# Where the gathered expert steps stand beside the dense top-16 searches

## The chip, the cores and the metric

The kernel runs as one program on 1 core of a Trainium2 chip. A core has five engines with a queue of instructions each: TensorE (PE in the profile, its weight loads PEld), VectorE (DVE), ScalarE (ACT), GpSimd (POOL) and SyncE (SP). 16 DMA engines move data beside them. An engine takes its instructions strictly in their written order and waits on semaphores, so a wait also holds back all that stands behind it. The metric is the device time of one execution in microseconds.

## The reference

One layer of a diffusion backbone runs over 128 context tokens and 512 latent tokens of width 1024, five tiles of 128 tokens. A token mixer comes first. The change lies in the second half of the layer, PEER, a retrieval over 16384 one-neuron experts:

```
q = (xb @ w_query).reshape(t, 8, 2, 128)                  # 8 heads
s = einsum('thik,hink->thin', q, sub_keys)                # 2 x 128 scores a head
v_half, i_half = top_k(s, 16)                             # top 16 of each half
cand = v_half[:, :, 0, :, None] + v_half[:, :, 1, None, :]
top_v, top_pos = top_k(cand, 16)                          # top 16 of the 256 sums
idx, g = <expert numbers>, softmax(top_v)
act = gelu(einsum('thkd,td->thk', expert_u[idx], xb))
out = einsum('thk,thkd->td', g * act, expert_v[idx])
```

So each token has 128 picks: 8 heads of 16. The result is normalised, gated and added to the token.

## The kernel before, in words

**Two ways of doing the picks.** The context tile (tile 0) and latent tiles 1 and 2 (`APART`) are *gathered*. For every pick, GpSimd issues an indirect DMA that brings one row of `expert_u` for each of the 128 tokens (128 x 4 KB, 0.524 MB), VectorE takes its dot product with the token (`u_dot`), and later the row of `expert_v` comes and VectorE adds it, weighted (`v_add`). Latent tiles 3 and 4 (`WHOLE`) are *dense*. TensorE multiplies them with all of `expert_u`, streamed by SyncE as 128 blocks of 0.524 MB (`s_block`), ScalarE applies the gelu and stores (`take_s`). The gates are then built as a matrix from one-hot rows (`build`: `equal`, `weigh_i`, `build_unit`, `gate_unit`, 64 units), and TensorE multiplies with the blocks of `expert_v`.

**Steps.** The gathered tiles 1 and 2 have 2 x 128 picks. Step j of `apart_steps` on VectorE takes the dot product of pick j and, from j = 40 (`APART_LEAD`), adds the v row of pick j - 40. At j = 40, 56, 72, ... it also runs `weights` for a head, which needs ScalarE's `gates`. ASTEPS is 296. GpSimd's `rows_of_apart` issues the gathers in the same order: u row j, then v row j - 40. A row waits for its buffer: picks 0 to 31 use eight u buffers in turn; from pick 32 there are four for u rows and four for v rows. For row 32 GpSimd also waits until the context output has been stored (`out_done`), because two of the later buffers lie where that output was.

**Searches.** `top(...)` on VectorE does two top-16 searches. For head h the pair (3 * PH + h, 4 * PH + h) are the dense tiles; `topw_done` tells that all eight are finished. For gathered tiles it takes two heads at a time and releases 32 rows to GpSimd (`topk_done`). Pairs (0, 1) and (2, 3) stand between the dense searches (`APART_TOP_BESIDE`), later ones within the steps (`APART_TOP_AT`; pair (4, 5) at step 50).

**The written order around the change.** On VectorE:

```
for h in range(PH):
    top(3 * PH + h, 4 * PH + h)
    context_steps(CTX_BESIDE[h])
    if h in APART_TOP_BESIDE: top(...)
    if h == 6: result(0, pv_c, row(3, 0), 1, 0)
    apart_steps(APART_BESIDE[h])
apart_steps(SOFTMAX_AT)                  # 8
weigh_whole()
apart_steps(APART_EARLY - SOFTMAX_AT)
dve.wait_ge(s("tw_out"), 1)
build()
```

`result` finishes the context tile (L2260 to L2262) and lets ScalarE store it. ScalarE's `store(0, 1)` stands behind the take of dense block 24. `weigh_whole` normalises the dense softmax weights. It needs the exponent that ScalarE takes of them (`ew_done`, L1601 and L1602), and TensorE needs it in turn: behind dense block 46 stands `turn_tables` (L1160), which waits on `gw_done`. Behind the take of block 48 ScalarE copies the turned tables (`tw_out`). The first `equal` of the build also needs dense block 59, the build's matmuls all 64.

TensorE alternates between two banks for the dense blocks: block n waits until ScalarE has taken block n - 2. SyncE loads into six block buffers: block n is loaded once block n - 6 has been multiplied. Context picks have the same two kinds of steps (`context_steps`); their last five stand behind head 3's search.

`START_1`, the number of steps ahead of the build, is `sum(APART_BESIDE) + APART_EARLY`. From it follow the places of the later steps, of ScalarE's gates and of the second half's multiplications.

Of the kernel before, what the change touches and what calls it, by code (L numbers as in the profile page):

```python
# [184 lines left out]
ROW_NUMBER = {row: n for n, row in enumerate(ROW_ORDER)}  # L185
ASTEPS = 2 * PICKS + APART_LEAD
CTX_BESIDE = (5, 5, 5, 5, 0, 0, 0, 0)
APART_BESIDE = (0, 0, 0, 0, 8, 8, 8, 8)
APART_TOP_BESIDE = {2: (0, 1), 6: (2, 3)}
APART_TOP_AT = {16 * n - (7 if n == 6 else 14): (n, n + 1) for n in range(4, 2 * PH, 2)}  # L190
APART_EARLY = 42
SOFTMAX_AT = 8
UNITS = 64
UNIT = 4
# [21 lines left out]

START_1 = sum(APART_BESIDE) + APART_EARLY
START_BETWEEN = START_1 + sum(APART_BUILD)
# [95 lines left out]
def layer_kernel(nc, a, outs):  # L314

    y_out, st_out = outs
    with ExitStack() as ctx:
# [131 lines left out]
        def row(kind, t):  # L449
            return rows[kind][1 if t else 0]  # L450
# [47 lines left out]
        def s(name):  # L498
            if name not in S:
                S[name] = sem(name)  # L500
            return S[name]
# [705 lines left out]
        def _(act):  # L1207
# [345 lines left out]
            def tile_norm(n, src, out):  # L1553

                ch(A(out, src, ACT.Square, accum_out=pstat[:, n, 0:1]))
                A(pstat[:, n, 1:2], pstat[:, n, 0:1], ACT.Sqrt, bias=eps[:], scale=1.0 / D).then_inc(s("pv_done"), 1)
# [3 lines left out]
            def store(t, turn):  # L1560
                act.wait_ge(s("out_ready"), turn)
                nc.scalar.dma_start(yv[:, t, :], x1(t)).then_inc(s("out_done"), 16)
# [18 lines left out]
            def take_s(n, i):  # L1581

                act.wait_ge(s("s_full"), n + 1)
                if i >= HALF:
                    act.wait_ge(s("av_done"), i - HALF + 1)
                elif i == 32:
                    act.wait_ge(s("topw_done"), 2 * PH)
                elif i == 48:
                    act.wait_ge(s("u_used"), PICKS + 30)
                A(Aw[:, i % HALF, :], bank[4 + n % 2][:, 0:2 * P], ACT.Gelu_apprx_tanh).then_inc(s("s_out"), 1)  # L1590

            for n, i in enumerate(FIRST_ORDER):
                take_s(n, i)
                if n == 8:
                    act.wait_ge(s("vc_used"), PICKS)
                    tile_norm(0, pv_c, h2c)
                if n == 24:
                    store(0, 1)
                if n == 31:
                    act.wait_ge(s("topw_done"), 2 * PH)  # L1600
                    A(iotas, iota.unsqueeze(2).broadcast_to([P, P, UNIT]), ACT.Copy)  # L1601
                    A(d_w, d_w, ACT.Exp).then_inc(s("ew_done"), 1)  # L1602
                for item in APART_GATES.get(("first", n), []):
                    gates(item)
                if n == 48:
                    act.wait_ge(s("tw_full"), 1)
                    A(turned_i, bank[6][:, 0:2 * P], ACT.Copy)
                    A(turned_w[:, 1, :], bank[6][:, 2 * P:], ACT.Copy)
                    A(turned_w[:, 2, :], bank[7][:, 0:2 * P], ACT.Copy).then_inc(s("tw_out"), 1)
# [183 lines left out]
        def _(dve):  # L1793
# [521 lines left out]
# [3 lines that stand above are left out]
                if h in APART_TOP_BESIDE:  # L2318
                    top(*(PH + n for n in APART_TOP_BESIDE[h]))
                if h == 6:  # L2320
                    result(0, pv_c, row(3, 0), 1, 0)
                apart_steps(APART_BESIDE[h])
            apart_steps(SOFTMAX_AT)
# [3 lines that stand above are left out]
# [74 lines left out]
```

## Time and profile before

| | |
|---|---|
| median of 3 runs | 2661.77 us (2661.74 to 2667.35) |
| profiled execution | 2663.96 us, its span 2662.2 us |
| mean granted TensorE clock | 0.946 of full speed |
| TensorE busy | 2308.1 us (87%) |
| VectorE busy | 1822.3 us (68%) |
| GpSimd busy | 1164.0 us (44%) |
| ScalarE busy | 616.5 us (23%) |
| DMA | 702.71 MB, mean 264 GB/s |

The span runs from the first to the last instruction of the profiled execution; the execution's own time is a little longer than that. Busy shares are averages over stages with different limits. Times in the rows below are microseconds from the span's start. In a row in order of time the first number is when the instruction started and the second how long it was busy; in brackets stand the idle time of its engine just ahead of it and what ended that idle time.

### The profile page before, as it was taken

The numbers are of one execution on the slowest core, as the hardware profiler recorded it, in microseconds if no ns is written. First come the engines' busy times: TensorE is split into PE (matmuls) and PEld (weight loads), VectorE is DVE, ScalarE is ACT, GpSimd is POOL, SyncE is SP. The second block draws the span as 40 slices with busy tenths as digits, with TensorE's granted clock in tenths as the row PEclk, the third lists the DMA queues.
The fourth block names the chain that finished last, engine by engine and source line by source line (L and its number), as shares of the span: only waits on it lengthen the run. The fifth ranks groups of instructions, "written<-read, shape, count | busy, mean of one in ns | idle before, by whom it ended". The sixth has DMA issues, their size and how long they took to land.

```text
span 2662.2 us, 26319 instructions
## 1 busy us (share of the span) xinstructions
PE 2308.1 (87%) x8735; PEld 1447.0 (54%) x8735; DVE 1822.3 (68%) x3244; ACT 616.5 (23%) x1503; POOL 1164.0 (44%) x960
## 2 busy tenths in 40 slices
PE   6998888898999997999989989646899999999920
PEld 1344455444566543477578878546566666544400
DVE  2656776743100789787778996899767576767698
ACT  2215263421211113311421112168111011100010
POOL 0011222311000347676542336553547868776675
PEclk8999999999999998999999999878999999999965
DMA  9421110115184678999764779976999999999997
GB/s 361 143 79 40 32 50 31 55 40 173 64 279 163 214 302 332 352 399 415 273 259 174 267 260 362 349 278 210 357 419 383 394 378 419 355 419 392 410 388 291
DMA packets 235150, 702.71 MB, mean 264 GB/s; under 512 B 21008, under 2 KB 45712, under 8 KB 233616
## 3 DMA queue, kind: packets, MB, share of 16 engines
q0 software_dynamic: 115200, 419.48, 41.4%
q1 hardware_dynamic: 119104, 279.06, 28.3%
q10 hardware_dynamic: 720, 2.62, 0.2%
q8 instruction: 63, 1.03, 0.1%
q14 instruction: 63, 0.52, 0.1%
HBM read 687.98 MB, written 13.11 MB: 263 GB/s over the span
## 4 chain that ended last, share of the span: by engine, by line
PE 31%; DVE 26%; POOL 14%; DMA 14%; issue 11%; ACT 3%; SPq 1%; DVEq 0%; ACTq 0%; POOLq 0%
PE bank L933 12%; DMA arena<-in_peer_v,arena 7%; POOL arena L1730 6%; POOL arena L1722 6%; PE bank L779 4%; DMA arena<-in_peer_u,arena 4%; DVE arena L2143 4%; DVE arena L2121 3%; PE bank L825 2%; DVE arena L1908 2%; PE bank L1083 2%; DVE arena L2067 2%; POOL arena L1776 2%; PE bank L734 2%; DVE arena L2064 2%
## 5 line engine op out<-in xcount | busy, mean ns | idle before, releaser
L1722 POOL DMA_INDIRECT arena<-in_peer_u,arena x384 | 500.9, 1304 | 728.0 <-DVE arena L2121 384.2
L2143 DVE SCALAR_TENSOR_TENSOR arena<-arena 128x1024 f32<-128x1024 f32 x381 | 497.5, 1306 | 137.2 <-DMA arena<-in_peer_v,arena 132.0
L2121 DVE CUSTOM_DVE_ANT_0 arena<-arena 128x1024 f32<-128x1024 f32 x384 | 474.4, 1242 | 152.1 <-DMA arena<-in_peer_u,arena 151.8
L1730 POOL DMA_INDIRECT arena<-in_peer_v,arena x384 | 451.7, 1176 | 245.2 <-DVE arena L2143 138.5
L933 PE MATMUL bank<-arena 128*128 128x512 f32 (+1 forms) x1472 | 504.6, 504 | 14.2 <-DMA arena<-in_w_in 5.1
L1153 PE MATMUL bank<-arena 128*128 128x256 f32 x2048 | 455.2, 380 | 10.8 <-ACT arena L1590 10.0
L1184 PE MATMUL bank<-arena 128*128 128x512 f32 x1024 | 453.7, 596 | 7.7 <-DMA arena<-in_peer_v 4.5
L1153 PEld LDWEIGHTS bank<-arena 128*128 128x128 f32 x2048 | 390.1, 191 | 92.2 <-issue 41.4
L933 PEld LDWEIGHTS bank<-arena 128*128 128x128 f32 x1472 | 280.6, 192 | 233.9 <-issue 199.7
L1184 PEld LDWEIGHTS bank<-arena 128*128 128x128 f32 x1024 | 195.5, 191 | 227.9 <-issue 219.3
L779 PE MATMUL bank<-arena 128*128 128x512 f32 x384 | 187.3, 636 | 5.3 <-ACT arena L1263 3.9
L1590 ACT ACTIVATE arena<-bank 128x256 f32<-128x256 f32 x128 | 48.8, 383 | 589.4 <-PE bank L1153 575.5
L1695 POOL TENSOR_TENSOR arena<-arena 128x512 f32<-128x512 f32 x40 | 43.6, 1090 | 269.1 <-ACT arena L1311 269.1
L1171 PE MATMUL bank<-arena 128*128 128x128 f32 x512 | 81.1, 316 | 79.5 <-ACT arena L1626 79.5
L779 PEld LDWEIGHTS bank<-arena 128*128 128x128 f32 x384 | 75.3, 205 | 90.5 <-issue 88.8
L1108 PE MATMUL bank<-arena 128*128 128x256 f32 x512 | 114.1, 384 | 8.2 <-ACT arena L1516 8.2
L1171 PEld LDWEIGHTS bank<-arena 128*128 128x128 f32 x512 | 72.1, 221 | 88.8 <-issue 44.5
L1908 DVE SCALAR_TENSOR_TENSOR arena<-arena,convw_sb 128x644 f32<-128x644 f32 x96 | 101.5, 1058 | 12.4 <-DVE arena L1906 2.0
L1108 PEld LDWEIGHTS bank<-arena 128*128 128x128 f32 x512 | 98.0, 193 | 21.9 <-issue 7.7
L1311 ACT ACTIVATE arena<-bank,arena 128x128 f32<-128x128 f32 x320 | 86.9, 393 | 46.7 <-PE bank L875 46.2
L1626 ACT ACTIVATE arena<-arena 128x128 f32<-128x128 bf16 x256 | 83.3, 401 | 42.3 <-DVE arena L2287 42.3
L1279 ACT ACTIVATE arena<-bank 128x512 f32<-128x512 f32 x60 | 35.2, 597 | 224.5 <-PE bank L933 218.1
(252 smaller groups left out, 2352.5 us busy)
## 6 DMA issues: line engine op xcount, KB each, us to landing
arena<-in_peer_ut SPq DMA_DIRECT2D x128, 512.0 KB, 6.5
arena<-in_peer_v SPq DMA_DIRECT2D x128, 512.0 KB, 6.5
arena<-in_w_in SPq DMA_DIRECT2D x22, 2048.0 KB, 9.1
arena<-in_w_ada SPq DMA_DIRECT2D x8, 2048.0 KB, 12.0
arena<-in_w_ssd_out SPq DMA_DIRECT2D x8, 2048.0 KB, 13.4
arena<-in_w_query SPq DMA_DIRECT2D x8, 2048.0 KB, 8.0
arena<-in_w_ada_t POOLq DMA_DIRECT2D x16, 512.0 KB, 4.5
arena<-in_w_fourier SPq DMA_DIRECT2D x4, 2048.0 KB, 7.6
```

The lines of the kernel that those rows point to most:

```text
L779: mm(bank[2][:, :], w[:, k, c0:c0 + P], hT[:, k, P:TOK], start=(k == 0), stop=(k == KT - 1), skip_group_check=True)
L933: last = mm(bank[q % 5][:, 0:cols], rows_of(k), w[:, k, :], start=(k == 0), stop=(k == k_tiles - 1))
L1108: last = mm(bank[n % 4][:, 0:2 * P], w[:, k, c0:c0 + P], h2Tp[1 - pair][:, k, :], start=(k == 0), stop=(k == KT - 1))
L1153: last = mm(bank[4 + n % 2][:, 0:2 * P], ut[:, k, :], h2Tp[1][:, k, :], start=(k == 0), stop=(k == KT - 1))
L1171: last = mm(bank[GATE_BANKS[u % 6]][:, P * t:P * t + P], hot_j[u % HOTS][:, t, :], hot_i[u % HOTS][:, t, :], start=True, stop=True)
L1184: last = mm(bank[2 * t + half][:, :], Aw[:, i % HALF, t * P:t * P + P], v[:, 512 * half:512 * half + 512], start=(i == 0), stop=(i == NKEY ...
L1311: last = A(Ee[:, e % 4, j, :], bank[d][:, j * P:(j + 1) * P], ACT.Exp, bias=ncs[:, c, ds(g * HG + 32 * d + 4 * hq + j, 1)])
L1722: nc.gpsimd.indirect_dma_start(rowbuf[slot], None, a["peer_u"], bass.IndirectOffsetOnAxis(ap=entries(IDX, k), axis=0)).then_inc(row_in[slo ...
L1730: nc.gpsimd.indirect_dma_start(rowbuf[slot], None, a["peer_v"], bass.IndirectOffsetOnAxis(ap=entries(IDX, k), axis=0)).then_inc(row_in[slo ...
L1908: last = STT(o, cin[:, i % 2, k:k + 644], w(k), o, ALU.mult, ALU.add)
L2121: V.tensor_tensor_reduce(out=rowbuf[slot], in0=rowbuf[slot], in1=h2c if item < PH else h2a[:, item // PH - 1, :], scale=1.0, scalar=0.0, o ...
L2143: STT(pv, rowbuf[slot], w, pv, ALU.mult, ALU.add).then_inc(s("vc_used"), 1)
```

## The change

Three tables of the order of work and one condition change. Four gathered steps move behind head 3's dense search and two more behind each of heads 4 to 7; 12 fewer stand behind the dense searches. The second gathered pair of heads, (2, 3), is searched at head 5 instead of head 6. ScalarE takes the dense exponent behind its take of block 39 instead of block 31. `SOFTMAX_AT` stays 8, so `weigh_whole` stands behind step 51 where it stood behind step 39. The sum `START_1` stays 74.

```diff
-APART_BESIDE = (0, 0, 0, 0, 8, 8, 8, 8)
-APART_TOP_BESIDE = {2: (0, 1), 6: (2, 3)}
+APART_BESIDE = (0, 0, 0, 4, 10, 10, 10, 10)
+APART_TOP_BESIDE = {2: (0, 1), 5: (2, 3)}
 APART_TOP_AT = {16 * n - (7 if n == 6 else 14): (n, n + 1) for n in range(4, 2 * PH, 2)}
-APART_EARLY = 42
+APART_EARLY = 30
...
-                if n == 31:
+                if n == 39:
                     act.wait_ge(s("topw_done"), 2 * PH)
                     A(iotas, iota.unsqueeze(2).broadcast_to([P, P, UNIT]), ACT.Copy)
                     A(d_w, d_w, ACT.Exp).then_inc(s("ew_done"), 1)
```

## Rows read from the trace of the kernel before

**Rows 1.** busy time by stretch (busy us and instructions of each engine, granted clock, DMA)

```profile
1558.00:1610.00 52.00, 41.97 (x186) 36.06 (x185) 49.93 (x141) 11.02 (x21) 15.85 (x11) 0.93 0.62 215
...
1752.00:1860.00 108.00, 73.70 (x468) 65.45 (x469) 107.53 (x219) 91.48 (x299) 41.13 (x32) 0.89 0.64 217
1860.00:2330.00 470.00, 459.69 (x1601) 303.04 (x1600) 327.98 (x558) 55.56 (x128) 321.80 (x255) 0.99 0.98 386
```

**Rows 2.** the same view, stretches beside and without dense block loads

```profile
1630.00:1671.00 41.00, 41.00 (x194) 36.12 (x193) 26.08 (x34) 7.63 (x18) 33.70 (x23) 1.00 1.03 418
1691.00:1713.00 22.00, 18.41 (x86) 15.86 (x84) 20.55 (x27) 2.30 (x6) 17.56 (x15) 1.00 0.90 310
1713.00:1751.00 38.00, 0.00 (x0) 0.00 (x0) 33.42 (x44) 0.00 (x0) 29.94 (x27) 0.50 0.99 365
```

**Rows 3.** order of time, ScalarE (start us, us, what, idle before and releaser)

```profile
1575.61 0.38 ACTq L1562 DMA_DIRECT2D y_out<-arena  x1
1576.05 0.66 ACT L1590 ACTIVATE arena<-bank 128x256 f32<-128x256 f32 x2 [13.85 <-DVE arena L2262]
1582.09 0.38 ACT L1590 ACTIVATE arena<-bank 128x256 f32<-128x256 f32 x1 [5.38 <-PE bank L1153]
...
1600.73 0.63 ACT L1601 ACTIVATE arena<-shape_consts 128x512 bf16<-128x512 f32 x1 [4.44 <-DVE arena L2109]
...
1709.44 0.38 ACT L1590 ACTIVATE arena<-bank 128x256 f32<-128x256 f32 x1 [3.07 <-PE bank L1153]
1752.15 4.91 ACT L1626 ACTIVATE arena<-arena 128x128 f32<-128x128 bf16 x16 [42.33 <-DVE arena L2287]
```

**Rows 4.** order of time, TensorE

```profile
1649.88 0.82 PE L1160 MATMUL bank<-shape_consts,arena 128*128 128x128 f32 x6
...
1753.56 6.67 PE L1171 MATMUL bank<-arena 128*128 128x128 f32 x40 [44.15 <-ACT arena L1626]
```

**Rows 5.** order of time, VectorE (L2121 dot product, L2143 add, L2063 search, L2287 build)

```profile
1489.30 1.28 DVE L2143 SCALAR_TENSOR_TENSOR arena<-arena 128x1024 f32<-128x1024 f32 x1 [1.74 <-DMA arena<-in_peer_v,arena]
...
1584.66 0.29 DVE L2063 MAX8 arena<-arena 128x8 f32<-128x128 f32 x1
...
1600.61 1.22 DVE L2121 CUSTOM_DVE_ANT_0 arena<-arena 128x1024 f32<-128x1024 f32 x1
...
1609.77 1.22 DVE L2121 CUSTOM_DVE_ANT_0 arena<-arena 128x1024 f32<-128x1024 f32 x1
...
1629.88 1.23 DVE L2121 CUSTOM_DVE_ANT_0 arena<-arena 128x1024 f32<-128x1024 f32 x1 [2.10 <-DMA arena<-in_peer_u,arena]
...
1668.41 1.23 DVE L2121 CUSTOM_DVE_ANT_0 arena<-arena 128x1024 f32<-128x1024 f32 x1
...
1690.85 1.22 DVE L2121 CUSTOM_DVE_ANT_0 arena<-arena 128x1024 f32<-128x1024 f32 x1
...
1751.65 0.41 DVE L2287 TENSOR_TENSOR arena<-arena 128x512 bf16<-128x512 bf16 x1
```

**Rows 6.** order of time, GpSimd (L1722 gathers of u rows, L1730 of v rows)

```profile
1483.67 1.93 POOL L1730 DMA_INDIRECT arena<-in_peer_v,arena  x1 [32.38 <-DVE arena L2143]
1485.90 1.08 POOL L1722 DMA_INDIRECT arena<-in_peer_u,arena  x1 [0.30 <-issue]
...
1537.33 1.99 POOL L1722 DMA_INDIRECT arena<-in_peer_u,arena  x1 [0.30 <-issue]
...
1543.15 0.94 POOL L1722 DMA_INDIRECT arena<-in_peer_u,arena  x1 [0.30 <-issue]
...
1604.92 1.15 POOL L1722 DMA_INDIRECT arena<-in_peer_u,arena  x1 [14.41 <-DVE arena L2121]
...
1690.01 1.74 POOL L1722 DMA_INDIRECT arena<-in_peer_u,arena  x1 [15.34 <-DVE arena L2121]
```

**Rows 7.** DMA issues, 1476 to 1500 us, then 1540 to 1610 (median us to landing)

```profile
arena<-in_peer_u,arena POOLq DMA_INDIRECT x8, 8.8
...
y_out<-arena ACTq DMA_DIRECT2D x1, 512.0 KB, 2.6
```

## The prediction

> **What bounds the kernel now.** I read the page first, then the stretches around the change, then each engine's order of time there. The page's busy shares mix stages, so the stretches say more. After 1752 us the engines build the gates (VectorE 107.5 of 108 us busy), then come 470 us at a DMA share of 0.98 [rows 1]. All work after 1752 us is in the same order with and without the change, for START_1 stays 74 (32 + 42, then 44 + 30), and every later index derives from it. So the change is worth what it moves the start of the build, and a shift there reaches the end whole.
>
> What ends last before the build? ScalarE takes the last dense block at 1709.44 and then idles 42.3 us for VectorE [rows 3]; TensorE idles 44.2 us with it [rows 4]. VectorE is the late one: its first `equal` runs at 1751.65, right after step 73 of the gathered tiles [rows 5]. Dense work has 42 us to spare, VectorE none.
>
> VectorE is late because its rows are. From 1600.61 on, nine dot products (steps 24 to 32) run without a wait, one each 1.145 us (9.16 over 8). After them each waits: step 40 starts at 1629.88 and step 50 at 1668.41 [rows 5], 3.85 us a step for 2.4 us of work. In that time the DMA moves 418 GB/s, one 0.524 MB dense block each 3.45 us plus two gathered rows a step, with VectorE busy 26 of 41 us [rows 2]. Ahead of it, from 1558 to 1610, the DMA share is only 0.62 [rows 1]. That hole is what earlier steps could fill.
>
> **The change, part by part.** Twelve steps go ahead of or between searches: four to head 3, two more each to heads 4 to 7. Eight steps then remain before `weigh_whole` as before, so it runs after step 51 instead of after step 39; the top search of step 50 (16 us) now stands ahead of it too. The GpSimd queue issues its gathers in an unchanged order. No instruction is added or removed.
>
> *Head 3, steps 0 to 3.* The last context add ends at 1490.6 [rows 5]. The first row gather is issued at 1485.90 and gathers of that stretch land 8.8 us after issue in the median [rows 7]. For the first I take 5.6 us, which is what the gather just ahead needed (issued 1483.67 [rows 6], added at 1489.30), for the next three one per 1.95 us (half the 3.85 to 3.9 us step). The fourth lands at 1497.3, so head 4's searches start near 1498.4: 7.8 us later, 4.6 of work and 3.2 of waiting. Bounds for the waiting: 0 (all landed) to 8 (8.8 us for the last, and its issue four places down).
>
> *Heads 4 and 5.* Ten steps with eight row buffers, a search of 16 us ahead of each. The ninth and tenth rows are issued while the first two are used, and must land in some 8 us; row 32 did that in under 5 us (issued 1604.92 [rows 6], used 1609.77 [rows 5]). Cost 2.3 us a head, no wait. The second gathered pair moves from head 6 to 5, but both places precede the context result, so it moves nothing else.
>
> *The context result and its store.* It had 16 steps ahead of it, now 24: 8 x 1.145 = 9.2, plus 3.2 = 12.4 us. Its store goes from 1575.61 to 1588.0. ScalarE is held there, behind dense block 24, and TensorE behind ScalarE, which idles 13.9 us now [rows 3] and 26.3 then. I cost this at nothing by itself: the 42 us of slack hide it, but it moves blocks 27 to 63 by 12.4 us.
>
> *Head 6, steps 32 and 33.* Row 32's buffer waits for the store to land, 2.6 us [rows 7]: about 1591. Issue takes up to 1.99 us beside dot products, 0.94 beside searches [rows 6]. I put the landing near 1597.5 and that of row 33 near 1599.5, so the head ends at 1600.7 against 1599.5 unhindered. Bounds 0 to 5 us.
>
> *Head 7.* A 15.95 us search (1584.66 to 1600.61 [rows 5]) ends the dense searches at 1616.6, before it was 1600.6. The exponent at block 39 runs at 1582.09 (the take of block 27 [rows 3]) + 12.4 + 12 x 3.453 = 1635.9, so it waits for nothing, where it waited 4.4 us. Steps 34 to 37 then run freely to 1621.2. Row 38 is issued at 1618.1 and lands near 1624.6, row 39 near 1626.7, row 40 near 1631. That is 1.3 us behind the present 1629.88. The steps that ran early have thus bought nothing by step 40: the hole is filled at one place and another opens under head 7's search, where only four buffers are left to prefetch into, instead of eight.
>
> *The new wait.* TensorE turns the weights after dense block 46 and needs `weigh_whole`. It passes there now at 1649.88 [rows 4]. With the change it ends block 46 at 1582.09 + 12.4 + 19 x 3.453 = 1660.1 (a take follows each 0.38 + 3.07 us). Steps 40 to 47 at 3.85 reach 1662; from there the blocks are held and steps 48 to 50 run at the 2.9 us of a time without blocks (38 us for 27 gathers is 1.41 each [rows 2]). Step 50 starts near 1667, works 2.4, searches 16.2, step 51 takes 2.4, the weights 1.2: 1689.2. TensorE stands 29 us there, with blocks 47 to 63, ScalarE's takes and every later block load queued behind it. Its slack becomes: 1689.2 + 1.2 for the turns + 17 x 3.453 = 1749.1, plus a restart. The restart is bounded by the present one, after the store: the next take waited 5.4 us where 3.07 is usual, 2.3 us more [rows 3]; if all of two blocks ran at half clock it is 7. I take 3: 1752.
>
> *Late steps.* Now VectorE needs 60.8 us from step 52 at 1690.85 to `equal` at 1751.65 [rows 5], with almost no block traffic. The first row that it needs from there is issued at 1690.01 [rows 6]. In the changed kernel it starts at 1689.2, but eleven block loads (53 to 63) fall into that stretch, over 11 x 3.453 = 38 us. A gather beside blocks takes 1.78 to 1.93 us (41 us for 23, or half a step), without them 1.47 (22 us for 15) [rows 2]. About 20 gathers x 0.4 = 7.5 us more. Below stands nothing (blocks hidden), above 11 x 1.27 = 14 us (every block's 0.524 MB at 418 GB/s added in full). I take 7.5, since the two mixed and unmixed rows are this very pair. 1689.2 + 60.8 + 7.5 = 1757.5.
>
> The Trainium skill (DMA: Bandwidth & Descriptors, Where 436 GB/s comes from) puts the HBM side of one core at about 358 GB/s. By it 38 gathers and 11 blocks (25.7 MB) would take at least 72 us here, and the build would start near 1761. The 418 GB/s over 41 us of this trace contradict it, and the row decides.
>
> **Sum.** The build starts at 1757.5, not 1751.65: +5.9 us, rounded 6. The profiled execution took 2663.96 us (span 2662.2), so 2670; that execution lies 2.2 us over the median of 2661.77, so against the median I say 2667.8 us, +0.22%.
>
> **Rivals.**
> *Issue, not traffic, sets the gathers (no change).* GpSimd is never idle for longer than its 0.30 us gap from 1690 on, and one gather takes 0.94 us beside searches and 1.99 beside dot products [rows 6]. If issue sets the rate, the late blocks are free: VectorE ends at 1750.0, TensorE at 1752, and the build starts at 1752, +0.5 us: 2662.3. Against it: beside blocks the issue itself lengthens, with VectorE less busy (26 of 41 us against 20.6 of 22). The Trainium skill (SBUF — State Buffer, SBUF: two separate sides) has VectorE lock GpSimd out of a shared port while it writes descriptors; by that rule this rival would be the likely one.
>
> *It is faster: the rows come ahead.* If steps 0 to 3, 32, 33 and 38 to 40 find rows landed, since fewer blocks have passed by then (3.6 blocks, 12.4 / 3.453, at 1.27 us are 4.6 us of traffic put off), the weights are ready near 1684. TensorE ends at 1747; if late blocks are hidden too, the build starts 5 us early: 2656.8. It decides only where the weights come before 1685, since TensorE has 63 us of work behind them whatever VectorE does.
>
> *It is much slower.* The late steps run at the mixed 3.85 us for all 22: 85 less the four buffered ones (4 x 1.45) is 79, the build starts at 1768, +16.5: 2678.
>
> *The move does nothing.* Steps before 40 are undone by waits, as above, and the new wait ends just with VectorE: within 2 us, 2662.
>
> **How the numbers follow.** Forecast 0.50, its own range +2 to +11 (2664 to 2673), of it 0.40 above 0.2%. 0.2% is 5.3 us, about what a measurement of this kernel tells from none. Issue-bound 0.20, all same. Nothing 0.05, same. Faster 0.15. Much slower 0.10, with its upper half beyond the range. Slower 0.50, same 0.35, faster 0.15. The range 2658 to 2675 leaves out about half of the faster case and most of the much slower one.
>
> **What would show it.** Right: the ScalarE store near 1588; exponent near 1636 without a wait; a TensorE gap of 25 to 32 us ahead of the turns of L1160; step 51 behind the search near 1688; last dense take near 1752, not 1709; `equal` near 1757. Wrong: a gap ahead of L1160 under 20 us (the weights come early, the faster case), late steps still at 2.8 us a piece beside block loads (issue-bound), or a difference that grows or shrinks after the build, which I hold to be none.

## The result: 0.57% slower, and the profile after

| | before | changed |
|---|---|---|
| median of 7 runs each, on one chip | 2661.77 us | 2677.43 us |
| ratio of the times, 95% interval | | 1.0057 [1.0041, 1.0073] |
| profiled execution, its span | 2663.96, 2662.2 us | 2676.04, 2674.1 us |
| `equal` of the build starts | 1751.65 us | 1767.01 us |
| last dense block taken | 1709.44 us | 1759.46 us |

The ratio is some 15 us where 6 were forecast. The direction is right, the size is not. In the trace the build starts 15.4 us later. 2.0 us of it were there before the change begins: the last context add ran at 1491.27 instead of 1489.30 [rows 5], with the same work ahead of it. So below I count from that add: 262.35 us to the build before, 275.74 now, 13.4 more. This needs care in the other direction too: 3.5 us come back behind the build (span less build start is 910.5 us before and 907.1 now), though the first multiplication with a v block follows 121.6 us behind `equal` in both.

ScalarE in order of time in the changed kernel: the context store, block takes, the exponent, the first take after the turns, the build.

```profile
1594.75 0.38 ACTq L1562 DMA_DIRECT2D y_out<-arena  x1
1595.18 0.66 ACT L1590 ACTIVATE arena<-bank 128x256 f32<-128x256 f32 x2 [30.75 <-DVE arena L2262]
...
1642.95 0.62 ACT L1601 ACTIVATE arena<-shape_consts 128x512 bf16<-128x512 f32 x1
...
1666.84 0.38 ACT L1590 ACTIVATE arena<-bank 128x256 f32<-128x256 f32 x1 [3.07 <-PE bank L1153]
1704.20 0.38 ACT L1590 ACTIVATE arena<-bank 128x256 f32<-128x256 f32 x1 [36.97 <-PE bank L1153]
...
1767.51 4.90 ACT L1626 ACTIVATE arena<-arena 128x128 f32<-128x128 bf16 x16 [7.67 <-DVE arena L2287]
```

TensorE in the same stretch.

```profile
1595.71 71.09 PE L1153 MATMUL bank<-arena 128*128 128x256 f32 x320 [24.79 <-ACT arena L1590]
1698.04 1.54 PE L1160 MATMUL bank<-shape_consts,arena 128*128 128x128 f32 x6 [31.23 <-DVE arena L2281]
1699.37 60.05 PE L1153 MATMUL bank<-arena 128*128 128x256 f32 x272
1768.91 6.85 PE L1171 MATMUL bank<-arena 128*128 128x128 f32 x40 [9.49 <-ACT arena L1626]
```

The new wait is there as forecast: TensorE stands 31.2 us ahead of the turns of L1160, for the weights of L2281, with its 17 last blocks behind it. They took 60 us, and the slack fell from 42.3 us [rows 3] to 7.7. It is still VectorE that ends last.

VectorE in order of time: last context add, steps 0, 2 and 3 and head 4's search, step 33 of head 6, the first step behind head 7, steps 38 to 40, step 50, the weights, step 52 and the first `equal`.

```profile
1491.27 1.28 DVE L2143 SCALAR_TENSOR_TENSOR arena<-arena 128x1024 f32<-128x1024 f32 x1 [1.58 <-DMA arena<-in_peer_v,arena]
1494.95 1.23 DVE L2121 CUSTOM_DVE_ANT_0 arena<-arena 128x1024 f32<-128x1024 f32 x1 [2.40 <-DMA arena<-in_peer_u,arena]
...
1498.64 1.27 DVE L2121 CUSTOM_DVE_ANT_0 arena<-arena 128x1024 f32<-128x1024 f32 x1 [1.22 <-DMA arena<-in_peer_u,arena]
...
1501.19 1.23 DVE L2121 CUSTOM_DVE_ANT_0 arena<-arena 128x1024 f32<-128x1024 f32 x1 [1.27 <-DMA arena<-in_peer_u,arena]
...
1502.34 0.29 DVE L2063 MAX8 arena<-arena 128x8 f32<-128x128 f32 x1
...
1607.77 1.23 DVE L2121 CUSTOM_DVE_ANT_0 arena<-arena 128x1024 f32<-128x1024 f32 x1 [2.74 <-DMA arena<-in_peer_u,arena]
...
1624.87 1.22 DVE L2121 CUSTOM_DVE_ANT_0 arena<-arena 128x1024 f32<-128x1024 f32 x1
...
1631.34 1.22 DVE L2121 CUSTOM_DVE_ANT_0 arena<-arena 128x1024 f32<-128x1024 f32 x1 [1.82 <-DMA arena<-in_peer_u,arena]
...
1635.31 1.23 DVE L2121 CUSTOM_DVE_ANT_0 arena<-arena 128x1024 f32<-128x1024 f32 x1 [2.73 <-DMA arena<-in_peer_u,arena]
...
1637.74 1.22 DVE L2121 CUSTOM_DVE_ANT_0 arena<-arena 128x1024 f32<-128x1024 f32 x1 [1.21 <-DMA arena<-in_peer_u,arena]
...
1675.91 1.23 DVE L2121 CUSTOM_DVE_ANT_0 arena<-arena 128x1024 f32<-128x1024 f32 x1
...
1697.56 0.42 DVE L2281 TENSOR_TENSOR arena<-arena 128x256 f32<-128x256 f32 x1
1697.90 1.22 DVE L2121 CUSTOM_DVE_ANT_0 arena<-arena 128x1024 f32<-128x1024 f32 x1
...
1767.01 0.41 DVE L2287 TENSOR_TENSOR arena<-arena 128x512 bf16<-128x512 bf16 x1
```

Steps taken early wait for their rows one by one, where none waited ahead of step 33 before. Counted from the last context add, step 40 is at 146.5 us instead of 140.6: 5.9 us later, although it has 1.1 us less work ahead of it (the weights now come later). Step 52 is 5.1 us later (206.6 against 201.55). The other 8.3 us arise in the late steps, from step 52 to `equal`: 69.1 us instead of 60.8.

Busy time by stretch: beside searches, beside blocks, TensorE's stand, late steps beside blocks.

```profile
1558.00:1610.00 52.00, 27.21 (x118) 23.35 (x117) 45.90 (x113) 5.60 (x12) 21.55 (x16) 0.77 0.61 217
1630.00:1671.00 41.00, 36.81 (x171) 32.06 (x169) 23.75 (x32) 10.75 (x20) 24.25 (x25) 1.00 1.02 404
1676.00:1698.00 22.00, 0.00 (x0) 0.00 (x0) 20.86 (x66) 0.00 (x0) 5.34 (x5) 0.50 0.46 189
1713.00:1751.00 38.00, 38.00 (x178) 33.45 (x177) 25.59 (x31) 7.25 (x16) 23.91 (x22) 1.00 1.03 418
```

The hole in the DMA share from 1558 to 1610 was to be filled by early steps; its share is 0.61 where it was 0.62 [rows 1]. A new hole stands at 1676 to 1698, where TensorE and the block loads stand still and the gathers follow them behind full buffers: GpSimd is busy 5.3 of 22 us, the DMA moves 416 GB/s or more until 1684 and nothing from 1688 to 1698, and the granted TensorE clock is 0.50, the lower of its levels. The stretch from 1713 to 1751 had VectorE 33.4 us busy [rows 2] and has it 25.6 now.

### The profile page after: what moved, and what is told of

It is laid out like the page before. It is cut to its first block, busy times and chain, and to the rows that moved or that the text cites. A ratio compares the mean times of both kernels' runs of the same rounds, so it can differ in the third digit from the quotient of the medians.

```text
span 2674.1 us, 26319 instructions
## 1 busy us (share of the span) xinstructions
PE 2311.1 (86%) x8735; PEld 1448.6 (54%) x8735; DVE 1824.4 (68%) x3244; ACT 617.4 (23%) x1503; POOL 1153.5 (43%) x960
## 3 DMA queue, kind: packets, MB, share of 16 engines
q8 instruction: 63, 1.03, 0.1%
## 4 chain that ended last, share of the span: by engine, by line
PE 30%; DVE 26%; DMA 17%; POOL 13%; issue 11%; ACT 3%; SPq 1%; DVEq 0%; ACTq 0%; POOLq 0%
PE bank L933 11%; DMA arena<-in_peer_v,arena 9%; POOL arena L1730 5%; POOL arena L1722 5%; DVE arena L2143 4%; DMA arena<-in_peer_u,arena 4%; PE bank L779 4%; PE bank L825 2%; DVE arena L1908 2%; DVE arena L2121 2%; PE bank L1083 2%; DMA arena<-in_w_ssd_out 2%; DVE arena L2067 2%; PE bank L734 2%; DVE arena L2064 2%
## 5 line engine op out<-in xcount | busy, mean ns | idle before, releaser
L1722 POOL DMA_INDIRECT arena<-in_peer_u,arena x384 | 490.9, 1278 | 742.7 <-DVE arena L2121 401.7
L2143 DVE SCALAR_TENSOR_TENSOR arena<-arena 128x1024 f32<-128x1024 f32 x381 | 497.5, 1306 | 138.8 <-DMA arena<-in_peer_v,arena 134.7
L2121 DVE CUSTOM_DVE_ANT_0 arena<-arena 128x1024 f32<-128x1024 f32 x384 | 476.6, 1248 | 152.8 <-DMA arena<-in_peer_u,arena 152.1
L1730 POOL DMA_INDIRECT arena<-in_peer_v,arena x384 | 450.4, 1173 | 251.2 <-DVE arena L2143 148.8
L2063 DVE MAX8 arena<-arena 128x8 f32<-128x128 f32 (+1 forms) x120 | 40.5, 338 | 67.0 <-ACT arena L1478 54.4
```

Of the source, the lines that this page charges most:

```text
L1722: nc.gpsimd.indirect_dma_start(rowbuf[slot], None, a["peer_u"], bass.IndirectOffsetOnAxis(ap=entries(IDX, k), axis=0)).then_inc(row_in[slo ...
L1730: nc.gpsimd.indirect_dma_start(rowbuf[slot], None, a["peer_v"], bass.IndirectOffsetOnAxis(ap=entries(IDX, k), axis=0)).then_inc(row_in[slo ...
L2121: V.tensor_tensor_reduce(out=rowbuf[slot], in0=rowbuf[slot], in1=h2c if item < PH else h2a[:, item // PH - 1, :], scale=1.0, scalar=0.0, o ...
L2143: STT(pv, rowbuf[slot], w, pv, ALU.mult, ALU.add).then_inc(s("vc_used"), 1)
```

## The experiments

All tables not shown in an edit are those of the kernel named. "Counted" means from the last context add of the same trace. "Late steps" are steps 52 to 73, up to the first `equal`. Ratios are to the kernel before on the same chip; 0.1% is 2.7 us. A counted mark comes from one profiled execution, a ratio from several timed ones.

### Which part costs: the parts one by one

**The searched pair and the exponent alone** (kernel before with the two other edits of the change).

```diff
-APART_TOP_BESIDE = {2: (0, 1), 6: (2, 3)}
+APART_TOP_BESIDE = {2: (0, 1), 5: (2, 3)}
...
-                if n == 31:
+                if n == 39:
```

> The kernel before with only the gathered pair (2, 3) at head 5 and the dense exponent behind block 39; no step is moved. All theories: nothing but up to 2 us at the weights, which wait for the exponent at about 1628 us while row 40 is awaited anyway: ratio 1.000 (0.999 to 1.001). A rival in which the later exponent or the earlier pair itself costs would show 1.002 or more.

1.0004 [0.9985, 1.0024]; build at 263.1 us counted (before 262.35). These two edits do nothing by themselves.

**The late weights alone** (kernel before, `weigh_whole` behind step 51, no step moved).

```diff
-SOFTMAX_AT = 8
+SOFTMAX_AT = 20
```

> The kernel before, with SOFTMAX_AT = 20 alone: the weights behind step 51 as in the changed kernel, all steps and searches at their old places. Traffic theory: TensorE stands some 40 us from 1650 to about 1691 us, 11 blocks are loaded beside the late steps, which take 7 to 8 us longer; build start 1759, ratio 1.003. Rival, issue sets the gathers: ratio 1.000. Rival, the stand is the whole loss: ratio 1.006.

1.0028 [1.0011, 1.0045]; build 265.7 counted, +3.3. TensorE in this kernel:

```profile
1692.84 1.54 PE L1160 MATMUL bank<-shape_consts,arena 128*128 128x128 f32 x6 [36.27 <-DVE arena L2281]
```

It stood 36 us, and the late steps took 68.8 us, 8.0 more than before. 4.7 us of that had come back ahead of step 52, of it 2.7 at steps 40 to 50: TensorE stopped at 1656.6 and left the last of them without block loads, and the ten took 35.8 us where they take 38.5.

The start of the build doesn't tell the whole loss here. ScalarE took the last dense block, multiplied by 1754.24, only at 1766.50, and VectorE lost 4.9 us in the build to it. ScalarE and then VectorE:

```profile
1766.50 0.38 ACT L1590 ACTIVATE arena<-bank 128x256 f32<-128x256 f32 x1 [15.29 <-remote]
```

```profile
1770.25 0.42 DVE L2301 TENSOR_TENSOR arena<-arena,bank 128x256 f32<-128x256 f32 x1 [4.94 <-PE bank L1171]
```

The first multiplication with a v block lies behind this stand. Counted, it is at 383.9 us before, at 397.3 in the changed kernel (+13.4) and at 392.2 here: +8.3, which fits the ratio (0.28% is 7.5 us) better than +3.3 does.

**The weights early in the changed kernel** (straight behind the searches, after step 43; no other edit).

```diff
-SOFTMAX_AT = 8
+SOFTMAX_AT = 0
```

> The changed kernel, with SOFTMAX_AT = 0: the dense weights are made behind step 43 instead of behind step 51 and the search at step 50. Steps and their places stay. Traffic theory: TensorE no longer stands 31 us at the turns (weights ready near 1655 us, TensorE there at 1667), its last 17 blocks stream during steps 48 to 57 and the search at step 50, where the DMA otherwise has nothing to do; the late steps shrink from 69 us back towards 61 and the build starts 7 to 8 us earlier than in the changed kernel, 7 to 8 us later than before: ratio to before 1.003. Rival, issue sets the gathers: late blocks are free, the TensorE stand costs nothing, ratio stays 1.006. Rival, the stand itself is the whole loss: ratio 1.000.

1.0016 [1.0, 1.0033]; build 264.7 counted: of 13.4 us more than before, 11.0 are gone, and the late steps are back at 59.4 us. The ratio fell with it, from 1.0057 and 1.0044 (two measurements of the changed kernel, the second below) to 1.0016, by 7.5 to 11 us. This profile too shows ScalarE standing ahead of the take of a last dense block, and a longer loss in the build. ScalarE and then VectorE in it:

```profile
1733.14 0.38 ACT L1590 ACTIVATE arena<-bank 128x256 f32<-128x256 f32 x1 [4.76 <-remote]
1766.15 0.38 ACT L1590 ACTIVATE arena<-bank 128x256 f32<-128x256 f32 x1 [32.63 <-issue]
```

```profile
1774.97 0.42 DVE L2301 TENSOR_TENSOR arena<-arena,bank 128x256 f32<-128x256 f32 x1 [7.66 <-PE bank L1171]
```

ScalarE stood 32.6 us with no recorded releaser, TensorE had ended block 63 by 1738.3, and VectorE then lost 7.7 us. Counted to the first multiplication with a v block, only 3.5 of the 13.4 us are gone in this profile (393.8); the profiled execution was itself 6.7 us over the median of this kernel's twelve. What ScalarE waited for was not found. Of the twenty profiles only this one and that of the late weights alone start the build's multiplications late, 9.4 and 6.7 us behind the first `equal` where the others have 1.9.

**No steps at head 3** (the changed kernel, the four steps behind the searches instead; weights still behind step 51).

```diff
-APART_BESIDE = (0, 0, 0, 4, 10, 10, 10, 10)
+APART_BESIDE = (0, 0, 0, 0, 10, 10, 10, 10)
...
-APART_EARLY = 30
-SOFTMAX_AT = 8
+APART_EARLY = 34
+SOFTMAX_AT = 12
```

> The changed kernel with head 3's four steps put back behind the searches: APART_BESIDE (0,0,0,0,10,10,10,10), APART_EARLY 34, SOFTMAX_AT 12, so that the weights stay behind step 51. It tells whether head 3's wait for its first rows (5.2 us of 9.8) is lost for good. Traffic theory as predicted: the wait goes, the 4.6 us of work come back later beside blocks as steps of 3.85 us, four of them 15 us in place of 9.8, less the late waits for rows 38 to 40 that it merely displaces; build start within 3 us of the changed kernel, ratio 1.005 to 1.006. Rival, waits between searches are pure loss: the build starts 5 us earlier, ratio 1.004.

1.0028 [1.0013, 1.0043]; build 267.7, late steps 68.2. By the profiles the four steps at head 3 cost 8.1 us in the changed kernel, more than their waits there (5.2 us); by the two ratios of the changed kernel it is 4 to 8.

**The four steps at head 3 alone** (eight a head behind it; weights behind step 39, exponent and pair as changed).

```diff
-APART_BESIDE = (0, 0, 0, 4, 10, 10, 10, 10)
+APART_BESIDE = (0, 0, 0, 4, 8, 8, 8, 8)
...
-APART_EARLY = 30
-SOFTMAX_AT = 8
+APART_EARLY = 38
+SOFTMAX_AT = 4
```

> Of the moved steps only head 3's four: APART_BESIDE (0,0,0,4,8,8,8,8), APART_EARLY 38, SOFTMAX_AT 4 (weights behind step 39 as before), exponent behind block 39, pair at head 5. If the first rows' waits (5.2 us) are loss that nothing gives back: from the last context add to the build 267 us against 262, ratio 1.002. If, as I predicted, an early step gains later what it loses in waits: 262 to 263 us, ratio 1.000.

1.0011 [0.9999, 1.0024]; build 265.45, +3.1, late steps 61.1. This kernel's weights, behind step 39, also waited 4.5 us for the exponent of block 39, which they don't in the changed kernel. How much of the 3.1 us that wait left is not told apart.

**Ten a head alone, twice** (none at head 3; weights behind step 39).

```diff
-APART_BESIDE = (0, 0, 0, 4, 10, 10, 10, 10)
+APART_BESIDE = (0, 0, 0, 0, 10, 10, 10, 10)
...
-APART_EARLY = 30
-SOFTMAX_AT = 8
+APART_EARLY = 34
+SOFTMAX_AT = 0
```

> Of the moved steps only the two more behind each of heads 4 to 7: APART_BESIDE (0,0,0,0,10,10,10,10), APART_EARLY 34, SOFTMAX_AT 0 (weights behind step 39 as before), exponent behind block 39, pair at head 5. The tenth row of a head waits 0.7 to 2.7 us in the changed kernel. If these waits are loss: 2 to 4 us, ratio 1.001 to 1.0015. If steps ahead of the searches pay by rows that come sooner: ratio 0.999.

> Ten steps behind each of heads 4 to 7 with the weights early, once more on another set of runs: 0.9988 was measured, its interval from 0.9972 to 1.0003. A true gain would show again as 0.9975 to 0.9995 (a build start 2 to 5 us sooner); its profile showed none (262.4 us from the last context add to the build in both), by which the ratio is 1.000.

0.9988 [0.9972, 1.0003], then 1.0007 [0.9993, 1.0021]: no change. Their profiles put the build at 262.4 and 255.2 us counted, 7.2 us apart for one and the same kernel. So a difference of a few microseconds between two single profiles proves nothing here without the ratio beside it. In both VectorE waited for the exponent behind step 39, in the first for 4.9 us, in the second for 7.5:

```profile
1635.87 0.42 DVE L2279 TENSOR_REDUCE arena<-arena 128x16 f32<-128x256 f32 x1 [7.51 <-ACT arena L1602]
```

With these tables the exponent behind block 39 is too late; ten a head with it left behind block 31 was not tried.

**Nine a head, twice** (none at head 3; weights behind step 39).

```diff
-APART_BESIDE = (0, 0, 0, 4, 10, 10, 10, 10)
+APART_BESIDE = (0, 0, 0, 0, 9, 9, 9, 9)
...
-APART_EARLY = 30
-SOFTMAX_AT = 8
+APART_EARLY = 38
+SOFTMAX_AT = 4
```

> Nine steps behind each of heads 4 to 7 instead of eight or ten: APART_BESIDE (0,0,0,0,9,9,9,9), APART_EARLY 38, SOFTMAX_AT 4, exponent behind block 39, pair at head 5. Nine steps run without a wait in the kernel before; the tenth waited. If only the tenth's wait costs: build start level with ten a head or 1 to 2 us sooner, ratio 0.998 to 1.000. If it doesn't matter where the steps stand: 1.000.

> Nine steps behind each of heads 4 to 7 once more, on another set of runs: 0.9984 was measured (0.9969 to 1.0000), with a build start 1.4 us sooner in its profile. By the profile: ratio 0.9995. A gain beyond noise would show as 0.9975 to 0.9990 again.

0.9984 [0.9969, 1.0], then 1.0004 [0.9985, 1.0023]. Nothing is shown to beat the kernel before.

**The changed kernel again**, on the chip of the next experiments.

> The changed kernel itself, to stand on the same chip and beside the same runs of the kernel before as the next three: ratio 1.0057 as first measured (1.004 to 1.007); from the last context add to the first build instruction 276 us, where the kernel before has 262.

1.0044 [1.0028, 1.006]; build 275.6 counted, late steps 68.85, waits between searches 10.3 us (10.2 the first time). Step 52, the late steps and the start of the build repeat within 0.3 us, step 40 within 1.0.

### Why the late steps take 69 us

I had put 7.5 us on the traffic of 11 block loads. The next kernels take from the changed kernel the bytes, the loads, the products, and both.

**Small late blocks** (blocks 53 to 63 loaded in 128 of 1024 columns, so that their products use old data).

```diff
-                sp.dma_start(blocks[B_SLOT[n]], src).then_inc(b_in[B_SLOT[n]], 16)
+                cols = 128 if 53 <= n < HALF else D
+                sp.dma_start(blocks[B_SLOT[n]][:, 0:cols], src[:, 0:cols]).then_inc(b_in[B_SLOT[n]], 16)
```

> The changed kernel, with the eleven dense blocks that are loaded after TensorE's stand (53 to 63) loaded in 128 of their 1024 columns, by as many DMAs with the same waits; the dense scores of those blocks are computed from what lies in the buffers. It takes away 5.0 MB of traffic beside the late steps and nothing else. Traffic theory: steps 52 to 73 shrink from 69 to 61 or 62 us, the build starts 7 to 8 us earlier, ratio 1.003. Rival, the late steps are long because of issue, or because TensorE and ScalarE work beside them: they stay at 69 us, ratio 1.006.

1.0028 [1.0012, 1.0044]; build 275.1 counted, late steps 67.8 us. The ratio is what the traffic theory named, the late steps are what the rival named; the question is about the late steps, so they decide. Row for 1713 to 1751:

```profile
1713.00:1751.00 38.00, 38.00 (x178) 33.48 (x177) 27.78 (x34) 7.24 (x16) 31.41 (x22) 1.00 0.92 313
```

The traffic fell from 418 to 313 GB/s, and still 22 gathers were issued in 38 us as before. GpSimd was busy 31.4 us with them instead of 23.9.

**No late loads** (blocks 53 to 63 signalled but not loaded).

```diff
+                if 53 <= n < HALF:
+                    sp.nop().then_inc(b_in[B_SLOT[n]], 16)
+                    return
```

> The changed kernel without the loads of dense blocks 53 to 63 (SyncE signals them without a transfer; their scores are computed from what lies in the buffers). Cutting their bytes to an eighth left the late steps at 67.8 us, with as many packets as before. If the dense queue's packets at all, or its bytes, lengthen the late steps: 61 to 62 us with no such packets, ratio 1.002 to 1.003. If it is TensorE and ScalarE working beside them, or the way gathers and VectorE fall together, not the loads: 67 to 69 us, ratio 1.004.

1.0024 [1.001, 1.0039]; build 271.0, late steps 67.1. The gathers in the groups by line over the late steps, first of the changed kernel, then of this one:

```profile
L1730 POOL DMA_INDIRECT arena<-in_peer_v,arena x22 | 25.1, 1141 | 11.6 <-DVE arena L2143 6.7 <-issue 4.9
L1722 POOL DMA_INDIRECT arena<-in_peer_u,arena x21 | 23.1, 1102 | 9.2 <-issue 4.9 <-DVE arena L2121 4.4
```

```profile
L1733 POOL DMA_INDIRECT arena<-in_peer_v,arena x21 | 28.5, 1355 | 6.4 <-issue 6.4
L1725 POOL DMA_INDIRECT arena<-in_peer_u,arena x21 | 26.9, 1281 | 6.4 <-issue 6.4
```

This is the reading that decides. With the loads, GpSimd waits 11.1 us for buffers, because rows land late (9.7 us after issue in the median), and one issue takes 1.12 us in the mean. Without them rows land in 5.8 us and it waits for no buffer, but an issue takes 1.32 us: GpSimd is busy for 54.4 of the 67.1 us, and 42 gaps of 0.30 us fill the rest. At the 1.16 us an issue of the kernel before it would have been some 61. So when one limit goes, the other has grown.

**Short late products** (blocks 47 to 63 with one of eight matmuls; loads whole).

```diff
-                for k in range(KT):
-                    last = mm(bank[4 + n % 2][:, 0:2 * P], ut[:, k, :], h2Tp[1][:, k, :], start=(k == 0), stop=(k == KT - 1))
+                ks = 1 if 47 <= n < HALF else KT
+                for k in range(ks):
+                    last = mm(bank[4 + n % 2][:, 0:2 * P], ut[:, k, :], h2Tp[1][:, k, :], start=(k == 0), stop=(k == ks - 1))
```

> The changed kernel with one of eight matmuls for each of dense blocks 47 to 63 (their scores are partial). All loads stay, and come faster since TensorE frees the buffers sooner. If loads lengthen the late steps: 67 us or more still, for the same bytes have to come in the same stretch. If TensorE's and ScalarE's work beside them does: 61 to 62 us. The last dense take comes near 1722 us instead of 1764 in both.

1.0049 [1.0031, 1.0068]; build 273.7, late steps 66.7, the last take at 1732.74. TensorE was idle for most of the stretch and 2.4 us were gained: it isn't TensorE that the late steps wait for. GpSimd's buffer waits were 9.8 us.

**Neither loads nor full products, twice** (both edits above together).

> The changed kernel without the loads of dense blocks 53 to 63 and with one of eight matmuls for blocks 47 to 63 (scores from what lies in the buffers, and partial). Either cut alone left the late steps at 67 us, once with buffers waited for and short gather issues (loads kept), once with no buffer waited for and long issues (products kept). If loads and the dense work each suffice to lengthen them: 60 to 62 us, ratio 1.001 to 1.002. If it is neither, and the place of the weights itself puts VectorE and GpSimd into a worse step with each other: 66 to 68 us again.

> The kernel of e13 once more, to see how far one profiled execution's late steps repeat: 64 to 67 us, issues 1.25 to 1.33 us in the mean, if 65.0 stands for the kernel; 58 to 62 if it was one draw among several.

Late steps 65.0 and 64.05 us, build 267.0 and 271.4 counted; ratios 1.0025 [1.0003, 1.0046] and 1.0025 [0.9999, 1.005]. Even with dense work all but gone, 3 to 4 us over 60.8 remain, and again it is the length of the issues. Groups by line of the first of the two:

```profile
L1726 POOL DMA_INDIRECT arena<-in_peer_u,arena x21 | 29.1, 1387 | 6.4 <-issue 6.4
L1734 POOL DMA_INDIRECT arena<-in_peer_v,arena x21 | 24.1, 1150 | 6.4 <-issue 6.4
```

**The same, with the weights earlier**: ahead of step 51, and behind step 43.

```diff
-SOFTMAX_AT = 8
+SOFTMAX_AT = 7
```

> The kernel of e13 with SOFTMAX_AT = 7: the weights directly behind the search at step 50, one step (2.4 us) earlier, so that no small instruction stands between steps 51 and 52. If their exact place decides: 58 to 61 us for steps 52 to 73. If any late place does, or none: 65 us.

```diff
-SOFTMAX_AT = 8
+SOFTMAX_AT = 0
```

> The kernel of e13 (changed; no loads of blocks 53 to 63, one of eight matmuls for blocks 47 to 63, so these scores are not the reference's) with SOFTMAX_AT = 0, the weights behind step 43. Late steps 52 to 73 have neither loads nor dense work beside them in either. If the weights between steps 51 and 52 put VectorE and GpSimd into the slower step (e13: 65.0 us, GpSimd's issues 1.27 us in the mean): 58 to 61 us and a mean of 1.05 to 1.15 here. If not: 65 us again.

Late steps 61.5 and 60.3 us, build 268.3 and 264.7; ratios 1.0019 [1.0001, 1.0037] and 1.0007 [0.999, 1.0024]. Groups by line of the one with the weights behind step 43:

```profile
L1726 POOL DMA_INDIRECT arena<-in_peer_u,arena x21 | 25.4, 1209 | 21.4 <-DVE arena L2125 15.3 <-issue 6.1
L1734 POOL DMA_INDIRECT arena<-in_peer_v,arena x21 | 23.0, 1095 | 6.4 <-issue 6.4
```

The 15.3 us are GpSimd's stand under the search, ahead of the stretch. The issues are back at 1.15 us in the mean. With the weights ahead of step 51 TensorE still stood 29.1 us, so its stand and restart are not what lengthens them. What differs is whether 1.1 us of VectorE work stands ahead of step 51 or behind it. But this is one profile, and the late steps of one and the same kernel lay 4.4 us apart (ten a head: 61.15 and 56.8), so 3 us for one step is not shown. What all profiles do show is weights ahead of step 44 with 56.8 to 61.7 us, and weights behind step 51 with 64 us or more whatever stands beside them.

Which issues are long can be read from the traces. Take the 823 gathers in the late steps of all twenty profiles that have a dot product or add of VectorE behind them, and for each the time from its start to the next start of such an instruction. All 141 issues of 1.5 us or more began at least 0.67 us ahead of it. Of the 420 that began less than 0.5 us ahead, none took over 1.37 us, and they took 0.99 in the mean. The gathers that began 0.7 us or more ahead number 14 in the kernel before, 16 in the changed one, 24 with small late blocks, 28 with none, 27 and 22 in the two of neither loads nor full products, 16 and 10 with the weights earlier. So the mean issue goes with how the two engines' starts fall together. Which of them puts the other there, and why it is so with late weights, is not shown.

**Dense work in the gap** (kernel before, with 96 more matmuls on old data behind block 63).

```diff
+            pe.wait_ge(s("s_out"), HALF)
+            for _ in range(12):
+                for k in range(KT):
+                    mm(bank[4][:, 0:2 * P], blocks[0].rearrange("p (k j) -> p k j", k=KT)[:, k, :], h2Tp[1][:, k, :],
+                       start=(k == 0), stop=(k == KT - 1))
```

> The kernel before, with 96 more matmuls (12 times the 8 of a dense block, out of a buffer that is there, results unused) after block 63, into the 42 us in which TensorE idled; no load, no wait and no VectorE or GpSimd instruction changes. If TensorE's work beside the gathers lengthens their issue: the late steps go from 60.8 to 64 to 67 us, ratio 1.002. If not: 61 us, ratio 1.000.

```profile
1724.37 41.71 PE L1196 MATMUL bank<-arena 128*128 128x256 f32 x192 [0.47 <-ACT arena L1595]
```

TensorE was busy until 1766, the late steps took 61.7 us: products alone don't lengthen them. The ratio was 1.0066 [1.0038, 1.0094], some 18 us, though. The profiled execution (2677.7 us, 12 under this kernel's median of 2689.7) shows no place for that, and it stays unexplained.

## Why the prediction was wrong in size

**Right.** The build's start decides and reaches the end nearly whole. The weights come behind step 51, TensorE stands 31.2 us for them (29 forecast), its 42 us of slack shrink to 7.7 (5.5 forecast), the exponent at 1642.95 waits for nothing, and VectorE still ends last. The pair and the exponent by themselves cost nothing (1.0004).

**The step that failed: the way to the weights.** I had step 52 at 1689.2, slightly ahead of the kernel before. It ran at 1697.90: 8.7 us late, of it 2.0 us of drift ahead of the change. Where they arose:

| | forecast | measured |
|---|---|---|
| waits at head 3 | 3.2 us | 5.2 us (9.8 from the add's end to the search, less 4.6 of work; 4.9 as the trace counts idle time) |
| waits of the tenth rows, heads 4 and 5 | 0 | 0.7 and 1.9 us |
| waits at head 6 | 1.2 us | 2.7 us |
| dense searches end | 1616.6 | 1624.87 |
| step 40 | 1631 | 1637.74 |
| step 50 | 1667 | 1675.91 |
| weights done, step 52 | 1689.2 | 1697.90 |

The waits between the searches were 10.2 us instead of 4.4, and the sentence "Cost 2.3 us a head, no wait" is the one that fell outright. The tenth rows were issued at 1521.76 and 1566.09, took 1.99 us to issue, and were used 7.6 and 8.8 us after the start of their issue; the "under 5 us" of row 32 did not hold for them. At head 3 the first row was issued at 1488.03 and used at 1494.95, 6.9 us later and not 5.6; the next three were issued 1.25 to 1.39 us apart and used 2.1 us apart in the mean, near the 1.95 forecast. So it was the first landing that was sized too small there.

Step by step: counted from the last context add, the searches end 6.3 us later than forecast (133.6 against 127.3). From there to step 40 the kernel took 12.9 us, 1.5 less than forecast: rows 38 to 40 waited 5.8 us, and step 38 waited for its buffer under the search, as I had said. Steps 40 to 50 then took 38.2 us instead of 36. So the claim that step 40 would run only 1.3 us behind the present one fell with the waits ahead of it, not with the buffers under head 7's search: counted it was 5.9 us behind, and nothing gave the lateness of heads 3 to 6 back. Of the 7.5 us between forecast (+5.9) and measured (+13.4), 6.7 are this way to step 52 and 0.8 the late steps. Last, the context result and its store came at 1594.75 instead of 1588.0, so TensorE ended block 46 at 1666.8 instead of 1660.1. Steps 40 to 48 took 3.96 us each (step 49 at 1673.38), and the "2.9 us of a time without blocks" came for the last one alone.

**The late term: the size nearly right, the reason wrong.** 60.8 + 7.5 = 68.3 was forecast and 69.1 measured. But the 7.5 us were to be traffic, 20 gathers by 0.4 us. (20 by 0.4 is 8, so the forecast sum was rounded down.) Taking the bytes of these loads away gave back 1.3 us, the loads themselves 2.0, the products 2.4, both 4 to 5, and both with the weights one step earlier 7.6. There are two limits of nearly the same rate. One is landing beside block loads, with GpSimd waiting for buffers. The other is the length of GpSimd's issues, which is 1.12 us in the mean in the changed kernel and 1.33 and 1.32 us in those with small late loads and none. My rival "issue, not traffic, sets the gathers" had half of it: without loads the issue does set the rate, in the kernel before too (48.20 us busy by the row below, and 42 gaps of 0.30 us, make 60.8). What it had wrong is that this makes the late blocks free. The kernel before over its late steps, busy time by stretch:

```profile
1691.00:1752.00 61.00, 18.41 (x86) 15.86 (x84) 54.97 (x72) 2.30 (x6) 48.20 (x43) 0.68 0.96 345
```

The Trainium skill (SBUF — State Buffer, SBUF: two separate sides) says that VectorE and GpSimd share a pair of SBUF ports which the one that starts first keeps for its whole instruction, and that GpSimd can't write descriptors while a VectorE instruction in a two-port mode holds them; two inputs in SBUF also make VectorE take the pair, against a GpSimd instruction that reads SBUF. The issues of 0.94 us beside searches and up to 1.99 us beside dot products [rows 6] agree with it, and so does the rule of starts above (none of 1.5 us or more among the 420). But beside dot products and adds, too, most issues are short: 32 of 43 took under 1.1 us in the changed kernel's late steps. That the port is the cause is not shown by these runs.

**Do the parts add up?** The kernels of the first section, with the start of the build and the first multiplication with a v block counted from the last context add:

| kernel | ratio | build | first v block |
|---|---|---|---|
| before | 1 | 262.35 | 383.9 |
| changed, twice | 1.0057, 1.0044 | 275.7, 275.6 | 397.3, 397.1 |
| late weights alone | 1.0028 | 265.7 | 392.2 |
| pair and exponent alone | 1.0004 | 263.1 | 386.6 |
| these two and head 3's four steps | 1.0011 | 265.45 | 387.5 |
| these two and ten a head, twice | 0.9988, 1.0007 | 262.4, 255.2 | 384.2, 377.8 |
| changed, weights early | 1.0016 | 264.7 | 393.8 |
| changed, none at head 3 | 1.0028 | 267.7 | 390.0 |

By the start of the build alone the parts seem to make half of the whole: +3.3 and +3.1 against +13.4. The other two columns don't bear that out, for the mark leaves out what the late weights cost behind it. By the ratios the late weights are 0.28% alone and 0.28 to 0.41% within the changed kernel, and the parts (0.28, 0.11, -0.12 or 0.07) sum to 0.27 to 0.46% (with pair and exponent in two of them) against 0.57 and 0.44, each known to some 0.15. Whether the whole is more than its parts is therefore not shown.

What differs between the two kernels with late weights can be read. With late weights alone TensorE stopped 14 us ahead of step 50 (1656.6 against 1670.7 there), and steps 40 to 50 gained 2.7 us. In the changed kernel TensorE is later by its longer hold at the context store and runs until 1666.8, 9 us ahead of step 50, of which only the last step became faster. The rest of its stand falls under the search of step 50, where VectorE needs no rows and GpSimd's buffers are full: the DMA moved 189 GB/s over those 22 us.

**The rivals.** Faster: its point was weights before 1685, they came at 1697.9. Much slower: 16.5 us was closest in size, but its mechanism (3.85 us a step to the end) is not what ran; late steps were at 3.1 us each. Nothing: no.

**Open.** Why more issues are long with late weights once the loads are gone; the stands of ScalarE, 32.6 us with early weights in the changed kernel and 15.3 us with late weights alone; the ratio of the kernel with dense work in the gap; and the 3.5 us that came back behind the build.

## What to carry to other kernels

A step moved into a place where its engine has no idle time gains only if its input is already there; price each moved step by issue, landing and buffer count, and assume that lateness stays unless a row shows who gives it back. A release point that is counted in steps (here `SOFTMAX_AT`) moves with the steps: moving it back alone recovered 7.5 to 11 us by the ratios, more than half of the loss. Look at a mark behind the one that you expect to decide: the start of the build showed 3.3 us of a loss of some 8. When taking one suspected limit away changes little, take the second away with it before acquitting either. And profile a kernel twice before you read 5 us from one trace.

## What the runs showed of the hardware

- A GpSimd gather of 128 rows takes 0.94 us to issue or up to 2.0, and the mean over some 42 of them ranged from 1.04 to 1.33 us in kernels whose VectorE work in that stretch was the same within 1 us (54.5 to 55.0). It was 1.07 to 1.19 us in the five profiles with whole late loads there, 1.04 to 1.18 in the eleven with the weights ahead of step 44 or (once) of step 51, where at most a part of the loads was left, and 1.25 to 1.33 in four with late weights and the late loads small or gone. The long issues began 0.67 us or more ahead of VectorE's next dot product or add, in all 141 cases.
- With both kinds of transfer the DMA moved 418 GB/s over 38 us; with small blocks it moved 313, and as many gathers were issued (22).
- ScalarE stood 32.6 us in one profile and 15.3 us in another ahead of the take of a block that had long been multiplied, while the DMA share was 1.03 and 1.02. That it waited for its own instructions to be fetched is a guess.
- Two profiles of one kernel differed by 7.2 us at the same mark (255.2 and 262.4), while its two ratios differed by 0.2%. Two of another differed by 4.4 us (267.0 and 271.4) at equal ratios.
